# Latent attention in a two-layer encoder: a head's scores issued ahead of the next head's query product, and its maxima ahead of that query's scaling

## What is computed

```python
q = (rms_norm(q_lat, q_norm) @ w_q_up).reshape(b, s, B_HEADS, B_NOPE + B_ROPE)      # 16 heads of 64 + 32
...
for i in range(s // Q_BLOCK):                                                       # 4 blocks of 128 queries
    logits = (einsum(q_nope, k_nope[:, :q1]) + einsum(q_pe, k_pe[:, :q1])) * scale  # keys up to the block's end
    logits = where(chunk_id[None, :q1] <= chunk_id[q0:q1, None], logits, -inf)
    probs = softmax(logits)
    outs.append(einsum(probs, v[:, :q1]))
```

## Time and profile before

| what | value |
|---|---|
| median of 3 runs | 1807.49 us (1806.69 to 1807.75) |
| profiled execution | 1805.97 us, span of the trace 1804.2 us |
| granted TensorE clock | 0.999 of full speed |
| busy: PE, DVE, ACT | 1787.3, 918.9, 621.2 us |
| the head loop | about 1290 to 1405 us of the span |

### The profile page before, as it was taken

One profiled execution on the slowest core, in us unless ns is written; L12 is line 12 of the kernel. 1 busy time (PEld: TensorE's weight loads), 2 busy tenths in 40 slices (PEclk: granted clock), 3 DMA queues, 4 the chain that ended last, 5 costly groups with the idle time before them and its releaser, 6 DMA issues.

```text
span 1804.2 us, 23133 instructions
## 1 busy us (share of the span) xinstructions
PE 1787.3 (99%) x8521; PEld 1465.4 (81%) x8521; DVE 918.9 (51%) x1393; ACT 621.2 (34%) x1054; POOL 140.7 (8%) x119
## 2 busy tenths in 40 slices
PE   8999999999999999999999999999999999999998
PEld 6888888887788888888888888888867788888887
DVE  5543443468654334445543443456897544344375
ACT  5322222347543223223332231233566443122222
POOL 0100100011011001010110010100000011010010
PEclk9999999999999999999999999999999999999999
DMA  6433333233333333333333333234112333333321
GB/s 180 119 93 94 103 95 90 85 110 90 87 104 95 97 95 100 94 88 98 106 93 99 94 98 95 88 95 123 27 41 62 94 94 116 93 95 103 93 94 58
DMA packets 316435, 170.50 MB, mean 95 GB/s; under 512 B 13330, under 2 KB 311503, under 8 KB 316367
## 3 DMA queue, kind: packets, MB, share of 16 engines
q1 hardware_dynamic: 314656, 167.07, 31.7%
q10 hardware_dynamic: 1710, 2.53, 0.5%
HBM read 163.03 MB, written 2.10 MB: 92 GB/s over the span
## 4 chain that ended last, share of the span: by engine, by line
PE 94%; DVE 2%; issue 1%; ACT 1%; DMA 1%; SPq 0%; POOL 0%; DVEq 0%; ACTq 0%; POOLq 0%
PE bank L1190 29%; PE bank L1191 29%; PE bank L1192 29%; PE bank L1447 2%; PE bank L1470 1%; PE bank L1459 1%; DMA w_raw<-ffn_gu 1%; ACT w_hi L569 0%; PE bank L1358 0%; PE bank L1328 0%; PE bank L1204 0%; DMA m_q<-work 0%; PE bank L1343 0%; DVE w_lo L794 0%; DVE xT L863 0%
## 5 line engine op out<-in xcount | busy, mean ns | idle before, releaser
L1190 PE MATMUL bank<-h_hi,w_hi 128*128 128x512 f32 x1520 | 594.5, 391 | 0.2 <-DVE h_lo L822 0.2
L1192 PE MATMUL bank<-h_hi,w_lo 128*128 128x512 f32 x1520 | 591.9, 389 | 0.0
L1191 PE MATMUL bank<-h_lo,w_hi 128*128 128x512 f32 x1520 | 591.7, 389 | 0.0
L794 DVE TENSOR_TENSOR w_lo<-w_raw,w_hi 128x1024 fp32r<-128x1024 f32 (+2 forms) x316 | 391.5, 1240 | 309.8 <-ACT w_hi L569 301.1
L569 ACT ACTIVATE w_hi<-w_raw 128x1024 fp32r<-128x1024 f32 (+2 forms) x316 | 317.0, 1004 | 287.6 <-PE bank L1192 271.1
L1190 PEld LDWEIGHTS bank<-h_hi,w_hi 128*128 128x128 f32 x1520 | 285.4, 188 | 59.8 <-DVE h_lo L822 0.6
L1192 PEld LDWEIGHTS bank<-h_hi,w_lo 128*128 128x128 f32 x1520 | 285.4, 188 | 59.7
L1191 PEld LDWEIGHTS bank<-h_lo,w_hi 128*128 128x128 f32 x1520 | 285.5, 188 | 58.1
L1190 PE MATMUL bank<-y_hi,w_hi 128*128 128x512 f32 x784 | 306.3, 391 | 0.7 <-DVE w_lo L794 0.7
L1192 PE MATMUL bank<-y_hi,w_lo 128*128 128x512 f32 x784 | 305.3, 389 | 0.0
L1191 PE MATMUL bank<-y_lo,w_hi 128*128 128x512 f32 x784 | 305.2, 389 | 0.0
(11 more groups left out here) (160 smaller groups left out, 1053.4 us busy)
## 6 DMA issues: line engine op xcount, KB each, us to landing
w_raw<-ffn_gu SPq DMA_DIRECT2D x176, 512.0 KB, 3.7
w_raw<-ffn_d SPq DMA_DIRECT2D x70, 512.0 KB, 3.9
w_raw<-ffn_d SPq DMA_DIRECT2D x24, 384.0 KB, 3.3
w_raw<-a_in SPq DMA_DIRECT2D x10, 512.0 KB, 3.9
w_raw<-a_out SPq DMA_DIRECT2D x8, 512.0 KB, 4.2
w_raw<-b_out SPq DMA_DIRECT2D x8, 512.0 KB, 3.7
w_raw<-b_in SPq DMA_DIRECT2D x5, 512.0 KB, 3.8
w_raw<-b_qup SPq DMA_DIRECT2D x16, 144.0 KB, 2.3
```

Of the source, the lines that this page charges most:

```text
L794: last = v.tensor_tensor(w_lo[:, sl, 0:k, 0:m], w_raw[:, sl, 0:k, 0:m], w_hi[:, sl, 0:k, 0:m].bitcast(F32), ALU.subtract)
L1190: t.matmul(b[:, :], wh, hi[:, c, :], start=c == 0, stop=False)
L1191: t.matmul(b[:, :], wh, lo[:, c, :], start=False, stop=False)
L1192: last = t.matmul(b[:, :], wl, hi[:, c, :], start=False, stop=c == k - 1)
```

## The change

Two calls trade places in the loop of PE, and two in the loop of DVE. PE now goes S(h), P(h+1), O, T(h-1) at head h, and DVE goes M(h), Q(h+1), `low`, probabilities, `pair_out`. Nothing else is altered: ACT, SP and POOL have the same instructions in the same order.

```diff
@@ -1119,9 +1119,9 @@
             low(n + AHEAD)
             scaled_q(0, n)
             for h in range(HEADS):
+                maxima(h)
                 if h + 1 < HEADS:
                     scaled_q(h + 1, n)
-                maxima(h)
                 if h + 1 < HEADS:
                     low(n + h + 1 + AHEAD)
                 probabilities(h)
@@ -1490,11 +1490,11 @@
             pe.wait_ge(misc_free, M_F)
             products(n, 0, lat_hi, lat_lo)
             for h in range(HEADS):
+                scores(h)
                 if h + 1 < HEADS:
                     products(n + h + 1, 0, lat_hi, lat_lo)
                 else:
                     out_part(out_b, PAIRS, 0, 5)
-                scores(h)
                 if h >= 4 and h % 2 == 0:
                     outputs((h - 4) // 2)
                 if h > 0:
```

## The result

The changed kernel takes 1809.52 us (median of 22 runs), the unchanged one beside it 1806.77 (22 runs): 2.75 us more, a ratio of 1.0016 with a 95% interval of 1.001 to 1.0022. (One of the 22 runs took 4681.78 us; the ratio is made without it.) The predicted change was +1.0 us, with +0.5 to +2.5 as its own range. So the sign and the place came out, and the size is nearly three times the forecast. The time lies within the stated range of 1806.8 to 1811.3 us, and even within the 1808.0 to 1810.0 given for this case, but the latter is luck: the forecast started from 1807.49 us, and the unchanged kernel, measured beside the changed one, takes 0.7 less. The change itself, 2.75, lies above the 0.5 to 2.5. It is also less than the 3.6 us that the prediction took for the least that can be told from no change; the runs here do tell it.

The account below looks back on a forecast made before the run. PE was taken as the bound, DVE close behind and setting the pace up to head 4. 0.71 at the start, 5 x 0.04 at odd and 6 x 0.02 at even heads made +1.0: 1808.5 us, range 1806.8 to 1811.3.

Parts of the forecast that it names:

- PE sets the pace from head 5 on, DVE up to head 4: Head loop before the change: DVE needs 5.89 us a head up to head 4; later PE is busy all 13.10 per pair.
- S(0) waits for Q(0), S(1) for Q(1): First heads: PE idles about 1.1 us before each; S(2) to S(4) wait for a Q behind the maxima.
- The start costs 0.7 us.: First heads: S(5) comes at 1320.24 against 1319.53, and this shift of 0.71 us is passed on to all behind.
- the same work in the same stretch: Last head: S(15) changes places with 15 matmuls of the output projection, which adds nothing to the time.
- The new loop S, P, Q, S: Later heads: the loop takes 5.36 us against PE's 5.32 at an odd head, costing 0.04 at each of five.
- Transposes followed by scores cost 0.09 more: Later heads: with 0.07 saved at the other seam, +0.02 us at each of six even heads, bounds -0.07 and +0.11.
- The upper end of the sum, 2.5: Whole kernel: both seams and the release at their upper ends, 0.71 + 0.16 + 5 x 0.2 + 6 x 0.11 us.
- the dearer release (0.16): End of Q to scores: upper bound 0.4 us, twice the weight load, instead of 0.24; enters the upper sum as 0.16.
- Rival 1: Heads 1 to 4: M half a microsecond earlier removes waits, seams save 0.07 at 11 heads; 0.8 us less, 1806.7; 8%.
- Rival 2: Later heads: O behind P makes `pair_out` late, delaying Q and S of odd heads; 5.1 us more, 1812.6; 9%.
- Rival 3: First heads: two PE pauses of about 1.1 us within 6.5 lower the clock; 2.5 us more, 1811.0; 4%.
- Rival 4: Whole loop: Q is released before PE finishes the transposes and the start evens out; within 0.3 of 1807.5 us; 12%.

Follow-up runs that it names:

- Experiments 5: Unchanged kernel with the low parts of twelve query weight blocks made on GpSimd instead of DVE: 1805.90 us against 1806.84, ratio 0.9996.
- 8: Unchanged kernel with head 0's `low` moved ahead of Q(1), into an idle stretch of DVE: 1806.49 us against 1806.84, ratio 0.9998.
- experiment 6: Changed kernel with the low parts of twelve query weight blocks on GpSimd instead of DVE: 1808.20 us, ratio 1.0008 to the unchanged kernel.
- experiment 3: Unchanged kernel with PE's half alone, S(h) ahead of P(h+1), DVE's order as before: 1839.93 us, ratio 1.0173.
- experiment 4: Unchanged kernel with DVE's half alone, M(h) ahead of Q(h+1), PE's order as before: 1823.57 us, ratio 1.0087.

## Why the prediction was right in sign and place, and short in size

- *PE sets the pace from head 5 on, DVE up to head 4.* Right for the unchanged kernel. Experiments 5 and 8 take away DVE's work and only the first heads get shorter.
- *S(0) waits for Q(0), S(1) for Q(1), about 1.1 us each, and S(2) to S(4) for a Q behind the maxima.* The waits are right in every instance, the first two being 0.95 long. Counted from the anchor the worked starts were S(4) 24.38 and S(5) 32.16 us, the trace has 24.14 and 32.04. S(1) was to come 0.2 us later and comes no later (6.47 after the anchor, before 6.50), for the reason given under the new loop below. M(4) was forecast half a microsecond earlier and is 0.52 earlier.
- *"The start costs 0.7 us."* This step failed. It took the shift of S(5) for the shift of all that follows. In the new order S(5) has one query product less ahead of it than in the old one, 9 matmuls at 0.23, 2.07 us. The starts of S were compared at places that stand behind different amounts of work. The same slip came back at the last head, where "the same work in the same stretch" overlooked that P(15) had been done before S(14) and now is not. With the product the worked starts give 0.71 + 2.07 = 2.8 us, and the first O shows 2.66. The two idle stretches of 1.1 us that the text itself had named were by themselves more than the 0.7; adding up PE's idle time would have shown it.
- *The new loop S, P, Q, S takes 5.36 us and costs 0.04 at each odd head.* Wrong, but small. It rested on 0.24 us from the end of Q to the scores. The trace has 0.06 (1289.72 to 1289.78), and 0.10 more is lost inside the scores. The row of the load and that of the matmul start together, at 1289.77 and 1289.78; where PE has work, the load leads by 0.11, as at S(5):

```profile
1289.77 1.60 PEld L1447 LDWEIGHTS bank<-kt,work 128*128 128x128 f32 x8 [1.21 <-DVE work L1069]
...
1320.53 1.60 PEld L1447 LDWEIGHTS bank<-kt,work 128*128 128x128 f32 x8
```

  So the hand-over costs about 0.16 us in all, and the loop 5.28 instead of 5.36. Between S(0) and S(1) it takes 5.29, and that is still under PE's 5.32 at an odd head. The Trainium skill ("TensorE: Matmul & The Clock Gate", section "Architectural detail: the array is 16× 32×32, not 1× 128×128") states that a matmul can begin before its weight load is complete. The starts in this trace agree, 0.01 us apart with a load of 0.19. But the 0.10 that the scores take longer may be the part of the load that is not hidden; no run separates it.
- *Transposes followed by scores cost 0.09 more.* Right: they cost 1.09 against 1.01, and scores followed by a product save 0.07, so a pair is 13.12 against 13.10. The measured price of all later heads is about 0.05 us, and the forecast had 0.3.
- *The upper end of the sum, 2.5.* It counts the dearer release (0.16) once at the start, where by its own chain two lie one behind the other up to S(2), before S(0) and before S(2). That makes 2.7. The term in question was too high all the same; what the sum lacked was the product.
- *Rival 1, the maxima's lead counts.* The lead is there and brings nothing: S waits for the Q behind it. With DVE relieved (experiment 6) the loss is still 2.4 us.
- *Rival 2, a late `pair_out`.* It does not occur. DVE has 11.85 of 13.12 us filled, and the 0.26 us worked out as free behind `pair_out` are there: M(5) starts at 1321.76 behind 0.27 us of idle time.
- *Rival 3, the clock falls.* Not in the changed kernel, where the granted clock is 1.00 between 1286 and 1300 us with 0.95 us idle twice. It does in experiments 3 and 4. Behind the nine waits of experiment 3 (3.10 us once, 2.02 eight times, in the trace's brackets) eight times work at the lowered clock follows; in experiment 4 it does behind the one wait of 2.50 at head 1, and the clock stays at 1.00 from 1330 to 1420 us, where waits of 1.41 recur at every odd head. So the risk was real. The waits of the changed kernel, 0.79 at most in brackets, are shorter than any behind which the clock fell in these runs; that they are few is not what saved it, since the 1.41 at every odd head cost no clock either.
- *Rival 4, the change does nothing.* It was wrong: the interval of the ratio, 1.001 to 1.0022, leaves out no change. The later heads do even out, the start doesn't.

## What to carry to other kernels

Two orders of one engine's work can be compared only at a place ahead of which the same work has been done in both; elsewhere the start of an instruction shows the shift plus whatever was moved across it, and the sum of the engine's idle time is the check. A product in hand, made one step ahead of its use, is what covers the hand-over to another engine and back; giving it up cost 2.4 to 2.7 us at the first steps here, where nothing else lies in the queue, and 0.4 later, where other work covers the way. When two engines' loops are written for each other, half of a reordering can cost many times the whole (33 and 17 us against 2.7).

## What was not expected of the hardware

In experiment 3 the lowered clock behind eight of nine pauses of 2.0 to 3.1 us costs 13.6 us, on top of the 18.4 of the pauses themselves. A weight load released by another engine delays the matmuls behind it by less than its own length: 0.06 us from the end of DVE's instruction to the start of load and first matmul, and 0.10 us lost within the scores, with a load of 0.19 us. And GpSimd took 0.82 and 0.39 us (mean of 12) for the two subtractions of a weight block (128x288 and 128x96) that take DVE 0.45 and 0.25, while DVE's reductions of the maxima beside it kept their mean of 489 ns.
